# Expert slots taken two at a time on every engine that works on them

## The reference, cut to what matters

```
def one_chunk(args):
    hc, ec, gc = args
    pre = jnp.einsum('cd,chkd->chk', hc, u[ec]).astype(jnp.float32)
    coef = (gc * jax.nn.gelu(pre, approximate=False)).astype(h.dtype)
    return jnp.einsum('chk,chkd->cd', coef, v[ec])
...
out = lax.map(one_chunk, (h.reshape(nchunk, TOK_CHUNK, d),
                          eidx.reshape(nchunk, TOK_CHUNK, PEER_HEADS, PEER_TOPK),
                          g.reshape(nchunk, TOK_CHUNK, PEER_HEADS, PEER_TOPK)))
```

## Time and profile before

| | |
|---|---|
| median of three runs | 2644.8 us (2644.13 to 2647.96) |
| the profiled execution, its own time | 2649.4 us |
| its span, first to last instruction | 2647.6 us |
| TensorE busy | 2197.7 us, 83% |
| VectorE busy | 1327.1 us, 50% |
| ScalarE busy | 1036.6 us, 39% (160 table loads among it) |
| GpSimd busy | 581.2 us, 22% |
| gathers | 512, 540 MB |
| mean granted TensorE clock | 0.89 of 2.4 GHz |

### The profile page before, as it was taken

One profiled execution on the slowest core, in us unless ns is written; L12 is line 12 of the kernel. 1 busy time (PEld: TensorE's weight loads), 2 busy tenths in 40 slices (PEclk: granted clock), 3 DMA queues, 4 the chain that ended last, 5 costly groups with the idle time before them and its releaser, 6 DMA issues.

```text
span 2647.6 us, 30679 instructions
## 1 busy us (share of the span) xinstructions
PE 2197.7 (83%) x10876; PEld 1328.3 (50%) x10876; DVE 1327.1 (50%) x3152; ACT 1036.6 (39%) x2580; POOL 581.2 (22%) x568
## 2 busy tenths in 40 slices
PE   5999999998777656555667876789999969999999
PEld 3877567777433112111124422356666637558888
DVE  7743744445766777777776555643334332101000
ACT  3124534423454444444446656645554232321000
POOL 0000000001343444444444223333333310000000
PEclk9999999999888777877678988899999989559999
DMA  8721011234899999999999888899999963004455
GB/s 335 271 72 48 0 40 56 64 97 146 354 420 421 419 421 413 421 413 419 415 404 397 318 325 298 309 395 409 412 411 411 418 258 119 17 0 129 153 156 151
DMA packets 124276, 710.51 MB, mean 268 GB/s; under 512 B 14648, under 2 KB 16824, under 8 KB 58464
## 3 DMA queue, kind: packets, MB, share of 16 engines
q0 software_dynamic: 74432, 540.07, 50.4%
q1 hardware_dynamic: 49456, 168.38, 18.4%
q10 hardware_dynamic: 240, 0.16, 0.0%
HBM read 706.45 MB, written 2.12 MB: 268 GB/s over the span
## 4 chain that ended last, share of the span: by engine, by line
PE 62%; DMA 20%; ACT 8%; DVE 5%; issue 3%; POOL 2%; ACTq 0%; SPq 0%; POOLq 0%; DVEq 0%
DMA arena<-experts,eidx 18%; PE psum L1046 11%; PE psum L850 11%; PE psum L595 5%; PE psum L596 5%; PE psum L597 5%; PE psum L1059 4%; DVE arena L1585 3%; PE psum L925 3%; PE psum L1028 2%; POOL arena L1560 2%; ACT L1299 1%; PE psum L707 1%; PE psum L973 1%; PE psum L972 1%
## 5 line engine op out<-in xcount | busy, mean ns | idle before, releaser
L850 PE MATMUL psum<-arena,sq 64*64 64x512 f32 x4096 | 640.4, 752 | 382.1 <-ACT sq L1309 360.9
L1585 DVE CUSTOM_DVE_ANT_0 arena<-arena 128x1024 f32<-128x1024 f32 x560 | 679.2, 1224 | 270.1 <-DMA arena<-experts,eidx 235.8
L1560 POOL DMA_INDIRECT arena<-experts,eidx x512 | 566.2, 1106 | 1031.6 <-PE psum L850 843.4
L850 PEld LDWEIGHTS psum<-arena,sq 64*64 64x64 f32 x4096 | 155.2, 157 | 778.4 <-ACT sq L1309 528.6
L1299 ACT ACTIVATE arena<-arena 128x1 f32<-128x1 f32 x512 | 103.0, 201 | 589.0 <-DVE arena L1585 579.7
L1046 PE MATMUL psum<-n_t,ring 128*128 128x256 f32 x1408 | 313.7, 382 | 1.7 <-DVE n_t L1582 1.7
L1046 PEld LDWEIGHTS psum<-n_t,ring 128*128 128x128 f32 x1408 | 264.5, 190 | 65.0 <-issue 30.5
L1309 ACT ACTIVATE sq<-sq,arena 128x64 f32<-128x64 f32 x512 | 178.1, 348 | 49.8 <-ACT arena L1303 2.2
L595 PE MATMUL psum<-hn_high,w_high 128*128 128x512 f32 (+1 forms) x432 | 178.9, 414 | 15.0 <-DVE hn_low L1582 13.6
L596 PE MATMUL psum<-hn_low,w_high 128*128 128x512 f32 (+1 forms) x432 | 173.5, 402 | 0.0
L597 PE MATMUL psum<-hn_high,ring_low 128*128 128x512 f32 (+1 forms) x432 | 172.3, 399 | 0.0
(11 more groups left out here) (271 smaller groups left out, 2810.1 us busy)
## 6 DMA issues: line engine op xcount, KB each, us to landing
ring<-w_stream SPq DMA_DIRECT2D x264, 512.0 KB
arena<-w_ada SPq DMA_DIRECT2D x48, 512.0 KB, 6.1
arena<-experts,eidx POOLq DMA_INDIRECT x512
x<-xT SPq DMA_DIRECT2D x1, 2048.0 KB, 15.0
arena<-rel_rows POOLq DMA_DIRECT2D x1, 2048.0 KB, 11.9
outT<-hn_rest SPq DMA_DIRECT2D x16, 128.0 KB
arena<-sub_keys POOLq DMA_DIRECT2D x1, 1024.0 KB, 6.4
arena<-cond SPq DMA_DIRECT2D x1, 512.0 KB, 4.2
```

The costliest lines, as they stand in the source:

```text
L850: last = mm(bank(4 + 2 * odd + a)[HALF * b:HALF * b + HALF, :], diag[k, s, :], rows[k, s, D + a * 512:D + (a + 1) * 512], start=c == 0, st ...
L1560: nc.gpsimd.indirect_dma_start(rows[:, s, :], None, experts, bass.IndirectOffsetOnAxis(ap=eidx[:, n // P % 2, n % P:n % P + 1], axis=0)).t ...
L1585: return V.tensor_tensor_reduce(out=out, in0=a, in1=b, scale=1.0, scalar=0.0 if op1 == ALU.add else TAKEN, op0=op0, op1=op1, accum_out=accum)
```

## The change

The slots are taken in pairs on VectorE and ScalarE too, and the ticks of a pair all stand behind its second slot, on all three engines. VectorE does both dot products, then both parts of the choice, then 2 or 3 ticks. ScalarE does one Gelu over two columns, two scalings and two diagonals, and then the rest. TensorE combines as before at the even slot, and its ticks move behind the odd one. The gathers, the number of buffers and the arithmetic are the same.

```diff
+def pair_ticks(n):
+    return ticks_at(n - 1) + ticks_at(n) if n % 2 else 0
...
-                for _ in range(ticks_at(n)):
+                for _ in range(pair_ticks(n)):
                     next(pair, None)
...
-            def diagonal(n):
+            def diagonals(n):
                 s = n % SLOT
-                act.wait_ge(pre_done.sem, pre_done.ready(n))
-                steps(op(pre[:, s:s + 1], pre[:, s:s + 1], ACT.Gelu))
+                act.wait_ge(pre_done.sem, pre_done.ready(n + 1))
+                steps(op(pre[:, s:s + 2], pre[:, s:s + 2], ACT.Gelu))
...
-                steps(op(coef[:, s:s + 1], pre[:, s:s + 1], ACT.Copy, scale=wgt[:, n // P % 2, n % P:n % P + 1]))
+                for c in range(2):
+                    k = (n + c) % P
+                    steps(op(coef[:, s + c:s + c + 1], pre[:, s + c:s + c + 1], ACT.Copy,
+                             scale=wgt[:, n // P % 2, k:k + 1]))
                 if n >= SLOT:
-                    act.wait_ge(rows_used.sem, rows_used.free(n, SLOT))
+                    act.wait_ge(rows_used.sem, rows_used.free(n + 1, SLOT))
...
-                op(diag[:, s, :], ident_pair, ACT.Copy, scale=coef[:, s:s + 1]).then_inc(diag_done.sem, 1)
+                for c in range(2):
+                    op(diag[:, s + c, :], ident_pair, ACT.Copy, scale=coef[:, s + c:s + c + 1]).then_inc(diag_done.sem, 1)
...
-                diagonal(n)
+                if n % 2 == 0:
+                    diagonals(n)
...
-                dots(n)
+                if n % 2 == 0:
+                    dots(n)
+                    dots(n + 1)
```

## The result

The changed kernel takes 2585.9 us (median of four runs, 2583.99 to 2590.67), the kernel before 2644.5 us beside it: a ratio of 0.978, 95% interval 0.9763 to 0.9797.

The account below looks back on a forecast made before the run. Gathers bound 700 to 1380 us; a path through several engines paced the attention; DMA and TensorE lay close together in the feed-forward. Terms -22 - 7 - 1 + 0.6 = -29 took 2644.8 to 2616 us, range 2594 to 2638.

Parts of the forecast that it names:

- the idle time of ScalarE that stays: Attention: of ScalarE's 48.9 us idle, the 26.1 for the maximum go and 22.8 stay in the sum.
- The attention, 22 us less: Attention stage, 1550 to 1695 us: ScalarE's account gives 122.5 us in place of 145; bounds 9 and 45 less.
- The new waits inside a pair: Attention, ScalarE: 4.6 us for normalizing after the exponential in 13 of 16 units, 6 for Gelu behind later dot products.
- The second estimate: Attention: the path through several engines takes 12.1 us over two pairs, 6.1 a pair, or 5.3 with combine at full clock.
- The feed-forward, 1 us less: Feed-forward, 1790 to 2080 us: combine's 1.31 us idle behind VectorE's multiplication goes, but only 1 us is gained.
- the DMA engines are full, so little of it comes back: Feed-forward: with a DMA share of 1.01, at most 412 GB/s becomes 418, worth 4 us; 1 was taken.
- Projection and values: 1425 to 1550 us: the same mechanism, but TensorE mostly bounds; half of 14.6 us idle goes, 7 us less.
- The end: At the very end of the gathers, the last pair comes later: 0.6 us more.
- The gathers take all they can: Rival, 12%: TensorE's clock stays up and the attention goes at the DMA's pace; 55 us less, 2590 us.
- The gathers start late: Rival, 10%: back-to-back dot products delay gathers; the attention's gain of 22 us becomes 5, 2633 us.
- The waits only move: Rival, 8%: exponential, reciprocal and normalizing run without slot work between; 19 us more in all, projection gains nothing, 2642 us.
- Slower: Rival, 9%: in the feed-forward a waiting tick holds both next slots; TensorE waits 2.0 us at 22 tiles, 2660 us.

Follow-up runs that it names:

- ticks_only: The kernel before with one edit: all ticks of a pair stand behind its odd slot, on all three engines; 2597.8 us, ratio 0.9807.
- ticks_even: The kernel before with the ticks of a pair bunched behind its even slot, between the two slots one combine needs; 2773.3 us, ratio 1.0467.
- warm_after: The changed kernel with six extra matmuls ahead of each combine from slot 328 to 362, to keep TensorE busy; 2589.7 us, ratio 0.978.
- dve_pairs: The kernel before with only VectorE working in pairs, its ticks behind the pair; ScalarE and TensorE unchanged; 2635.9 us, ratio 0.9956.
- half_before: The kernel before with half the bytes in each gather: only the u row is gathered, and combine reads it; 2471.3 us.
- half_after: The changed kernel with half the bytes in each gather: only the u row is gathered, and combine reads it; 2404.6 us.
- relu_after: The changed kernel with Relu in place of Gelu on the dot products, which takes table loads away; 2582.8 us, ratio 0.9763.
- warm_before: The kernel before with six extra matmuls ahead of each combine from slot 328 to 362, to keep TensorE busy; 2639.9 us, ratio 0.9984.

## Why the prediction was wrong in size

The direction, the mechanism and the stage were right: ticks_only and ticks_even show the path as the prediction told it. Two terms of the sum were too small, and the step that failed in the larger one is "the idle time of ScalarE that stays": of 48.9 us it let the 26.1 for the maximum go and kept 22.8, less 2.8 between the steps of a slot, and then it added 10.6 of new waits: 30.6 us. In slots 328 to 364 of the changed kernel ScalarE is idle for 16.1 us, new waits included.

**The attention, 22 us less: measured 40.5 and 43.3.** The account in the prediction was ScalarE's: busy time, less what goes, plus idle time that stays, plus new waits. In slots 328 to 364 the traces give 93.0 busy + 48.4 idle before, 84.8 + 16.1 changed. Against the account:
- Of the idle time I let the 26.1 us for the row maximum go, with 2.8 between the steps of a slot, and kept the rest. But 9.3 us of the rest were waits for the transposed unit, the same kind of wait one tick further on, and they went too. Before:

```profile
ACT w_rest L1442 <- PE psum L990: 6.6, 2, 3.3
...
ACT hn_rest L1442 <- PE psum L990: 2.7, 1, 2.7
```

- The new waits inside a pair were put at 10.6 us. They are 2.6 (normalizing for the reciprocal, 8 times) and 4.6 (Gelu for the dot products, 7 times), 7.2 in all. One reading was wrong: in the trace of the changed kernel the normalizing follows its exponential directly in 10 of the 16 units, not in 13 (before it was 4).
- ScalarE's busy time fell by 8.1 us, not by the 3.8 that the Gelus are worth in 18 pairs. Two scalings in a row, and two diagonals, overlap, 2.0 us each, and one table load of 1.3 us less falls in these slots. Its groups in the changed kernel, same slots:

```profile
L1319 ACT ACTIVATE sq<-sq,arena 128x64 f32<-128x64 f32 x38 | 11.2, 340 | 1.9
L1311 ACT ACTIVATE arena<-arena 128x1 f32<-128x1 f32 x38 | 9.2, 287 | 0.8
...
L1305 ACT ACTIVATE arena<-arena 128x2 f32<-128x2 f32 x18 | 3.7, 204 | 5.5 <-DVE arena L1596 4.6 <-ACT mix L1412 0.4 <-ACT w_rest L1453 0.2
```

38 diagonals of 340 ns are 12.9 us one by one and 11.2 as they lie. The second of a pair costs 0.25 us, not the 0.348 of the earlier trace rows, so 0.10 us are hidden. The Trainium skill (ScalarE: Activation LUTs, section "What ACT_TABLE_LOAD costs") puts the overlap of two such instructions in a row at about 93 ns. The trace agrees with that.

These three are 9.3 + 3.4 + 4.3 = 17.0 of the 18.5 us that were missing. A slip of the sum is small beside them: 1.96 less 1.62 over 20 pairs is 6.8, and less the 4.2 for Gelu it leaves 2.6, not 2.8.

The second estimate, the path of 12.1 us over two pairs, seemed to confirm 6.1 us a pair. It did so only because I took combine at 3.5 us, its length behind a long wait. I had written down that full clock gives 5.3, and chose the value that agreed. Measured are 5.6 and 5.45 a pair. In the traces 9 of 19 combines take 3.5 to 3.7 us before, and 6 of 19 take 3.2 to 3.7 in the changed kernel; the others take 1.95. The agreement of the two estimates was thus no evidence. That 5.6 lies between the two values of the path confirms it as little: in warm_after every combine takes 1.95 us and a pair still 5.6.

**The feed-forward, 1 us less: measured 7.4 and 8.0.** The mechanism was as described: in slots 384 to 480 TensorE's waits for the diagonals are 17.5 us before and 11.0 changed, and dve_pairs shows that VectorE's order was the cause. The step that failed was "the DMA engines are full, so little of it comes back". I read a share of 1.01 as full. At 407 GB/s there was room up to 418, and half_before shows that the gathers did not set the pace. That VectorE waited for rows in only 3.3 us of that stage would have told.

**The rest.** Projection and values: 7 forecast, 10.0 and 8.8 measured. The first 276 slots: 0, measured 1.0 less and 0.2 more. Slots 364 to 384 were not in the sum: 3.7 and 3.3 less. Slots 276 to 292 were not either: 2.7 and 1.1 more. The end: 2.2 us given back from slot 480 on, where the gathers bound (98.1 us, and 83.4 with half the bytes), in place of 0.6.

**The rivals.** *The gathers take all they can* named 2590 us and came nearest, but for the wrong reason in the attention: with half the bytes it takes 98.0 us as before (half_after), so the gathers did not set the pace; the DMA share of 1.00 there only looks like it. *The gathers start late*: half of it came true. In the attention 21 of 38 gathers begin during a dot product where 13 did, but they take 1.25 us in the mean where those took 1.58 (the others 0.95 and 0.94), and VectorE waits for rows only 3.6 us. *The waits only move*: they do in small, 7.2 us. *Slower*: it did not come; combine waits less in the feed-forward, not more. The 56 us that ticks_even loses there are another case, ticks between the two slots of a pair.

**What stays open.** How the last 6 to 9 us in the attention divide between the two halves of the pairing rests on single traces. What holds the attention of the changed kernel at 98 to 101 us is known only in part: neither the gathers (half_after) nor TensorE's work (warm_after), but something with the table loads in it (relu_after). And warm_before does not bound what the clock is worth in the kernel before, since 5 of its 19 combines still take more than 1.95 us.

## What to carry to other kernels

Where one engine needs the work of two slots at once, look for anything that stands between the two on the engines that feed it and that waits for that same engine. Here it cost a round trip for each such pair, and moving it behind the pair gave 34.6 us in the attention with the same work. Count over how many steps of the consumer each path closes, before and after, on every feeding engine, before you read busy shares: here no engine was full. And price a change by what is left when the waits are gone. Here a second kind of wait (9.3 us) went with the first, combine ran at the lower clock less often, and a DMA share near 1 was a bound only where somebody waited for the data.

## What the runs showed of the hardware

Extra matmuls made a stage faster, as far as single traces tell. With six more matmuls for each pair the attention of the kernel before fell from 141.4 to 131.0 us, at a granted clock of 0.90 in place of 0.81. Before, 9 of its 19 combines took 3.5 to 3.7 us; with the extra matmuls 5 took 2.4 to 3.7 us, and the others 1.95. The combine at 1602.01 us of the earlier trace rows took 3.48 us. TensorE had waited 4.33 us ahead of it, and to 1605.05 us the granted clock was 0.50, which is 1.2 of 2.4 GHz. The whole kernel was not to be told from before.

The DMA share doesn't tell whether the transfers are the bound. In the feed-forward it was 1.01 at 407 GB/s, where halving the bytes changed nothing, and 1.02 at 418 GB/s, where halving them gave 9 us. In slots 0 to 256 of the kernel before, halving them gave 148 us.

Two small ScalarE instructions in a row that don't wait for each other overlap: two of the 128x64 diagonals take 0.59 us together, and one alone takes 0.348.
